# Moving two transfers, one TensorE position and the second half's products inside the steps of a fused attention and RWKV stage

## The chip, the core and the metric

The kernel runs on one core of one Trainium2 chip. The metric is the device time of one launch in microseconds (us), of the only core. TensorE, VectorE, ScalarE, GpSimd and SyncE are called PE, DVE, ACT, POOL and SP, as in the profile; each executes its own list of instructions in order and waits for the others on semaphores.

## The reference, cut to what matters

The program is two transformer-like blocks over 2048 tokens of width 1024. The first block (`hybrid_layer`) normalizes x, multiplies by `w_in`, runs five mixers of 256 columns each, and ends in

```python
mixed = jnp.concatenate([y.astype(x.dtype) * jax.nn.silu(z) for y, z in branches], axis=-1)
return x + mixed @ w_out          # 2048x1280 @ 1280x1024, plus the old x
```

Two of the five mixers stand in the stage of this change. `forgetting_attention` ("Fox") is causal softmax attention with 4 heads of 64, over blocks of 128 queries, so that block k sees (k+1)*128 keys. `rwkv7_time_mix` is a recurrence over tokens,

```python
sa = jnp.einsum("bhvk,bhk->bhv", state, -kk_t)
state = (state * w_t[:, :, None, :] + sa[..., None] * (kk_t * a_t)[:, :, None, :]
         + v_t[..., None] * k_t[:, :, None, :])
```

which the kernel computes in chunks of 128 tokens: running sums of the log decay within the chunk (the "decay sums"), products of scaled rows, and the inverse of a triangular matrix in seven doubling levels. The second block is outside this change.

## The kernel before

The stage is `fox_rwkv_and_gating` (L1062). Its loop runs k from 0 to 17; each k is one **step**, a block in which all engines start together and that ends when all are done. In step k (2 <= k <= 15) these branches run side by side: `rwkv_front` of tile k, `rwkv_back` of tile k-1, `fox_attend` of query block k, `fox_prepare` and `sgu_tile` of tile k+1, `out_product` of tile k-2 (the product with `w_out`) and, up to k = 14, `out_turn` of tile k-1 (its transposes).

**The order of the work is written by hand.** Every branch is a generator per engine; it yields a number between 0 and 1 and then issues instructions. `together` (L162) always continues the branch with the smallest number. The numbers are places in the engine's list, not times: an engine executes its list strictly in that order and stops at each semaphore wait that is not yet met.

**The product** (`out_product`, L1360). For each half n of the 1024 columns, ten blocks j of 128 rows, and a = 0 (the high part of the weights, two 128x512 matmuls) or a = 1 (the low part, one matmul): 40 slices of 256 KB, each loaded by SP into one of five buffers `ow`. The load of slice q is issued when slice q-5 has been used (`o_used`). From step 3 on the first five slices have been loaded in the step before (`ow_ahead`). The places are given by `at(n, j, a)`; in steps 3 and later the first half lies at 0 to 0.025 for slices 0 to 5 and then at 0.08 to 0.38, the second half at 0.405 to 0.775. Each half ends with a DVE addition to the tile's x rows in `ox` (L1436). SP issues from the same loop, ahead of the load of a given slice, the store of the rows of the tile before (L1387, 512 KB) and, after a wait for that store, the load of the old x rows (L1391, 512 KB). The second DVE addition must be done before the transposes of `out_turn` at place 0.84 write the same bank (L1331).

**The RWKV front on PE** (`rwkv_front`, L2404, N = 76). Low-rank products at 8/N; the decay sums at 14/N (L2579 to L2584), which wait for `la_done`, signalled by DVE at 13/N (after L2498), which itself waits for a Tanh of ACT (L2444). ACT takes the exponentials of the sums at 15/N (L2453 to L2455), DVE makes the scaled rows at 17/N (L2509 to L2514), PE turns them from 20/N (L2590). The seven levels follow from place 0.447 on: level l at (34 + 5.5 l + d)/N, with first products at d = -0.6, an ACT copy (L2469) at d = 1.5 and second products at d = 2 (all L2564).

**Places between 14/N = 0.184 and 16/N = 0.211 on PE** hold work of other branches:

| place | work | waits for |
|---|---|---|
| 0.192 | logits of Fox head 1, piece 0 (L1679) | its bank |
| 0.200 | `rwkv_back`'s U products (L2699) | `r_done`, an ACT copy (L2644) at 0.150 |
| 0.208 | turn of head 0, piece 0 (L1703), in steps 12 to 15 only | `f_exps`, ACT's exponential of head 0 (L1619) at 0.175 |
| 0.209 | slice 12 (j = 6, a = 0) of the product (L1424, L1425) | its load |

In steps 9 to 11 (three pieces of 512 keys) the turn of piece 0 is at 0.214.

Of the kernel before, what the change touches and what calls it, by code (L numbers as in the profile page):

```python
# [1211 lines left out]
OUT_K = MIX1 // P  # L1212
# [147 lines left out]
def out_product(c, b, s, t, ahead):  # L1360


    tok = slice(t * P, (t + 1) * P)
    mS, x, wr, bank = b.mS, b.x, b.wr, b.bank
    arrived = (s.ow_in0, s.ow_in1, s.ow_in2, s.ow_in3, s.ow_in4)
    slices = [(n, j, a) for n in range(2) for j in range(OUT_K) for a in range(2)]
    halves = x[:].rearrange("p (n c) -> p n c", n=2)
    cols = lambda n: slice(n * 512, (n + 1) * 512)

    def at(n, j, a=0):  # L1370

        if n == 0 and j < 3 and ahead:
            return 0.0002 * j if (j, a) != (2, 1) else 0.025
        if n == 0 and ahead:
            return 0.08 + 0.3 * (j - 3 + 0.4 * a) / (OUT_K - 3)
        return 0.005 + 0.4 * n + 0.37 * (j + 0.4 * a) / OUT_K

    def sync(sp):
        yield 0.0
        if not ahead:  # L1380
            for q in range(OUT_SLOTS):
                weights(sp, q, arrived[q])
        for q in range(OUT_SLOTS, len(slices)):
            n, j, a = slices[q - OUT_SLOTS]
            yield at(n, j, a) + 0.004
            if q == OUT_K and t:
                sp.dma_start(b.x_out[(t - 1) * P:t * P, :], x[:]).then_inc(s.ox_stored, 16)  # L1387
            if q == OUT_K + 5:
                if t:
                    sp.wait_ge(s.ox_stored, 16)  # L1390
                sp.dma_start(x[:], b.x_old[tok, :]).then_inc(s.ox_in, 16)  # L1391

            sp.wait_ge(s.o_used, q - OUT_SLOTS + 1)
            weights(sp, q, arrived[q % OUT_SLOTS])
        yield at(1, OUT_K) + 0.02
        if t + 3 < TILES:
            sp.wait_ge(s.o_used, len(slices))
            for q in range(OUT_SLOTS):
                weights(sp, q, s.ow_ahead)
            yield 1.0  # L1400
            sp.wait_ge(s.ow_ahead, 16 * OUT_SLOTS)

    def weights(sp, q, signal):
        n, j, a = slices[q]
        sp.dma_start(wr[:, q % OUT_SLOTS].bitcast(F32), b.split_d[OUT_ROWS[j], a, :, cols(n)]).then_inc(signal, 16)

    def landed(pe, q):
        if not ahead:
            pe.wait_ge(arrived[q % OUT_SLOTS], 16 * (q // OUT_SLOTS + 1))
        elif q >= OUT_SLOTS:  # L1410

            pe.wait_ge(arrived[q % OUT_SLOTS], 16 * (q // OUT_SLOTS))

    def tensor(pe):
        for n in range(2):
            for j in range(OUT_K):
                q = (n * OUT_K + j) * 2
                yield at(n, j)
                if j == 0 and n == 1:

                    pe.wait_ge(s.o_added, 1)
                landed(pe, q)
                whi, wlo = wr[:, q % OUT_SLOTS], wr[:, (q + 1) % OUT_SLOTS]
                pe.matmul(bank, mS.hi[:, j], whi, start=(j == 0), stop=False)  # L1424
                pe.matmul(bank, mS.lo[:, j], whi, start=False, stop=False).then_inc(s.o_used, 1)  # L1425
                yield at(n, j, 1)
                landed(pe, q + 1)
                pe.matmul(bank, mS.hi[:, j], wlo, start=False, stop=(j == OUT_K - 1)).then_inc(s.o_used, 1)

    def vector(dve):  # L1430
        for n in range(2):
            yield at(n, OUT_K) + 0.01
            dve.wait_ge(s.o_used, 2 * OUT_K * (n + 1))
            if n == 0:
                dve.wait_ge(s.ox_in, 16)
            dve.tensor_tensor(halves[:, n], halves[:, n], bank, ALU.add).then_inc(s.o_added, 1)  # L1436

    return {"sync": sync, "tensor": tensor, "vector": vector}


# [963 lines left out]
def rwkv_front(c, B, s, proj, i):  # L2404
# [17 lines left out]
    N = 76.0  # L2422
# [136 lines left out]
    def blocks(pe, l, out, left, right, corner):  # L2559

        m = None
        for h in range(HEADS):
            for k, rows, cols in corner if l == LEVELS - 1 else HALVES:
                m = pe.matmul(out[rows, h * P + cols.start:h * P + cols.stop], left(h)[k, rows], right(h)[k, cols],  # L2564
                              start=True, stop=True)
        return m

    def tensor(pe):
        yield 6 / N
        pe.wait_ge(s.lows, 1)  # L2570
        pe.transpose(b1[0:RANK, 0:P], x[:, D_WLO:D_WLO + RANK], c.ident)
        pe.transpose(b1[0:RANK, P:2 * P], x[:, D_ALO:D_ALO + RANK], c.ident).then_inc(s.low_ps, 1)
        yield 8 / N
        pe.wait_ge(s.low_kept, 1)
        pe.matmul(b2[:, 0:GW], loT[:, 0], lo2[:, 0], start=True, stop=True)
        pe.matmul(b2[:, GW:2 * GW], loT[:, 1], lo2[:, 1], start=True, stop=True).then_inc(s.wa_ps, 1)
        yield 14 / N
        pe.wait_ge(s.la_done, 1)
        pe.matmul(b0[:, 0:GW], c.all[:, CENTRED], wa[:, 0], start=True, stop=True)  # L2579
        pe.matmul(b0[:, GW:2 * GW], c.all[:, CENTRED_BEFORE], wa[:, 0], start=True, stop=True)  # L2580
        for j in range(2):
            lj = wa[:, 0, j * P:(j + 1) * P]
            pe.matmul(b1[:, 2 * j:2 * j + 1], lj, c.upto[:, P // 2 - 1:P // 2], start=True, stop=True)
            m = pe.matmul(b1[:, 2 * j + 1:2 * j + 2], lj, c.after[:, P // 2 - 1:P // 2], start=True, stop=True)  # L2584
        m.then_inc(s.cums, 1)
        for j in range(2):
            yield (20 + j) / N
            pe.wait_ge(s.tilde, 1)
            for a in range(4):
                m = pe.transpose((b2, b1)[j][:, a * P:(a + 1) * P],  # L2590
                                 (tl01[:, a] if a < 2 else tl23[:, a - 2])[:, j * P:(j + 1) * P], c.ident)
            m.then_inc((s.turned_a, s.turned_b)[j], 1)
        for j in range(2):
            yield (25 + 4 * j) / N

            pe.wait_ge(s.kept_a, 1)
            pe.wait_ge(s.kept_b, 1)
            if j:
                pe.wait_ge(s.g_done, 2)
            for b in range(2):  # L2600
                for r in range(2):
                    o = slice(HD * r, HD * r + HD)
                    m = pe.matmul(B.big[:, r, b * GW:(b + 1) * GW], XT23[o, j, b],
                                  XT01[o, j].rearrange("p a t -> p (a t)"), start=True, stop=True)
                    if b:
                        m.then_inc(s.grams, 1)
        for l in range(LEVELS):
            yield level(l, -0.6 if l else 0)
            if l == 0:
                pe.wait_ge(s.g_done, HEADS)  # L2610
                pe.wait_ge(s.x_set, 1)
            else:
                pe.wait_ge(s.x_kept, l)
            blocks(pe, l, b0, lambda h: own[:, h], lambda h: X[:, h], [(LOW, HIGH, LOW)]).then_inc(s.p1, 1)
            if l:
                yield level(l, 2)
                pe.wait_ge(s.p1c, l)
                pe.wait_ge(s.xt_kept, l)
                if l < LEVELS - 1:
                    blocks(pe, l, b1, lambda h: XT[:, h], lambda h: Pm[:, h], None).then_inc(s.x_ps, 1)  # L2620
                blocks(pe, l, b2, lambda h: Pm[:, h], lambda h: XT[:, h], [(HIGH, LOW, HIGH)]).then_inc(s.xt_ps, 1)
# [1332 lines left out]
```

## Time and profile before

| | |
|---|---|
| median of 3 runs | 4982.17 us (4981.24, 4982.17, 5010.14) |
| profiled execution | 4980.74 us, span 4979.1 us, mean granted PE clock 0.865 |
| busy share of the span | PE 85%, PE weight loads 63%, DVE 53%, ACT 39%, POOL 15% |
| DMA | 585.32 MB, mean 118 GB/s |
| the stage's steps 0 to 15 | from 1239.8 us on; step 15 begins at 2383.7 us |

A row of a timeline is: start in us, duration in us, engine, line, operation, written and read tiles, shapes, count; in brackets the idle time before it on that engine and what ended it. "PEq L134" is the block boundary. `fox_big` is PSUM, `halves` the split weights of `w_out`. A row of a table of windows is: window and its length, then busy time and count per engine, the granted PE clock (1.00 is 2.4 GHz, 0.50 is 1.2 GHz), the DMA share and GB/s.

### The profile page before, as it was taken

The numbers are of one execution on the slowest core, as the hardware profiler recorded it, in microseconds if no ns is written. First come the engines' busy times: TensorE is split into PE (matmuls) and PEld (weight loads), VectorE is DVE, ScalarE is ACT, GpSimd is POOL, SyncE is SP. The second block draws the span as 40 slices with busy tenths as digits, with TensorE's granted clock in tenths as the row PEclk, the third lists the DMA queues.
The fourth block names the chain that finished last, engine by engine and source line by source line (L and its number), as shares of the span: only waits on it lengthen the run. The fifth ranks groups of instructions, "written<-read, shape, count | busy, mean of one in ns | idle before, by whom it ended". The sixth has DMA issues, their size and how long they took to land. (4 is left out here: it accounts for less than half of the span.)

```text
span 4979.1 us, 66174 instructions
## 1 busy us (share of the span) xinstructions
PE 4215.4 (85%) x23522; PEld 3122.5 (63%) x23522; DVE 2660.2 (53%) x5590; ACT 1936.3 (39%) x4022; POOL 735.7 (15%) x755
## 2 busy tenths in 40 slices
PE   7997998985688898889889999877888787877589
PEld 5885777775566666666668888833444444544467
DVE  3113444444666555555421111178889888888546
ACT  3112232323333333333311101035677767767721
POOL 3111111110100000000000000022223333434500
PEclk9998999996589898989899999966578887788789
DMA  5326666664466555545452212210000001010033
GB/s 181 125 113 221 208 214 212 213 216 145 154 206 205 192 188 167 175 159 162 126 178 85 83 66 72 63 52 19 20 20 20 20 20 39 20 39 18 32 140 114
DMA packets 293737, 585.32 MB, mean 118 GB/s; under 512 B 47944, under 2 KB 80364, under 8 KB 293244
## 3 DMA queue, kind: packets, MB, share of 16 engines
q1 hardware_dynamic: 293408, 581.10, 34.7%
q8 instruction: 187, 3.06, 0.2%
q14 instruction: 142, 1.16, 0.1%
HBM read 453.03 MB, written 127.94 MB: 117 GB/s over the span
## 5 line engine op out<-in xcount | busy, mean ns | idle before, releaser
L3059 PE MATMUL ds_big<-ds_ikT,ds_iqT 64*128 64x512 f32 (+3 forms) x608 | 383.2, 761 | 73.6 <-ACT ds_iqT L3036 53.9
L3526 POOL TENSOR_TENSOR ds_E<-ds_bT 128x256 f32<-128x256 f32 x112 | 72.1, 644 | 2380.9 <-ACT ds_bT L3495 2206.1
L301 PE MATMUL g_acc<-g_ws_hi,g_hT_hi 128*128 128x512 f32 (+1 forms) x1024 | 386.2, 377 | 0.0
L302 PE MATMUL g_acc<-g_ws_lo,g_hT_hi 128*128 128x512 f32 (+1 forms) x1024 | 384.6, 376 | 0.0
L303 PE MATMUL g_acc<-g_ws_hi,g_hT_lo 128*128 128x512 f32 (+1 forms) x1024 | 384.6, 376 | 0.0
L529 PE MATMUL mm_big<-mm_gw_hi,mm_ghT_hi 128*128 128x512 f32 (+1 forms) x768 | 319.8, 416 | 30.3 <-PEq L134 30.3
L3115 DVE TENSOR_SCALAR_CACHE_REDUCE ds_seen<-ds_eq,ds_num 128x2048 uint16<-128x2048 uint16 (+13 forms) x224 | 331.3, 1479 | 26.1 <-issue 4.2
L531 PE MATMUL mm_big<-mm_gw_hi,mm_ghT_lo 128*128 128x512 f32 (+1 forms) x768 | 301.4, 392 | 0.0
L530 PE MATMUL mm_big<-mm_gw_lo,mm_ghT_hi 128*128 128x512 f32 (+1 forms) x768 | 300.5, 391 | 0.0
L3155 ACT ACTIVATE ds_signs<-ds_lo,ds_at 128x2048 bf16<-128x2048 uint16 (+13 forms) x224 | 291.3, 1301 | 2.1 <-issue 0.7
L328 DVE COPY g_stage<-g_acc 128x512 f32<-128x512 f32 (+1 forms) x64 | 41.5, 649 | 459.2 <-PE g_acc L303 459.2
L3022 DVE SCALAR_TENSOR_TENSOR ds_score<-ds_rel,ds_iw,ds_score 128x512 f32<-128x512 f32 (+3 forms) x266 | 219.5, 829 | 54.9 <-ACT ds_rel L3043 37.8
L3059 PEld LDWEIGHTS ds_big<-ds_ikT,ds_iqT 64*128 64x128 f32 x608 | 108.2, 235 | 209.7 <-issue 84.1
L347 ACT ACTIVATE g_stage<-g_acc 128x512 f32<-128x512 f32 (+1 forms) x64 | 36.2, 565 | 502.4 <-PE g_acc L303 502.4
L3043 ACT ACTIVATE ds_rel<-ds_big 128x512 f32<-128x512 f32 (+3 forms) x304 | 162.5, 538 | 158.5 <-PE ds_big L3059 85.2
L3634 PEld LDWEIGHTS ds_big<-ds_E 128*128 128x128 f32 x896 | 134.4, 229 | 135.5 <-POOL ds_E L3533 72.6
L303 PEld LDWEIGHTS g_acc<-g_ws_hi,g_hT_lo 128*128 128x128 f32 x1024 | 193.3, 189 | 35.3
L302 PEld LDWEIGHTS g_acc<-g_ws_lo,g_hT_hi 128*128 128x128 f32 x1024 | 193.5, 189 | 34.8
L301 PEld LDWEIGHTS g_acc<-g_ws_hi,g_hT_hi 128*128 128x128 f32 x1024 | 193.5, 189 | 34.6
L3407 PE MATMUL ds_big<-ds_pT,ds_ct 128*128 128x128 f32 x1088 | 169.3, 300 | 53.7 <-ACT ds_pT L3317 53.5
L1635 ACT ACTIVATE fox_pT<-fox_big 128x512 f32<-128x512 f32 (+3 forms) x160 | 85.4, 533 | 323.3 <-PE fox_big L1703 323.1
L1031 PE MATMUL fp_acc<-fp_ws_hi,fp_hT_hi 128*128 128x512 f32 (+1 forms) x528 | 199.2, 377 | 8.8 <-issue 3.6
(550 smaller groups left out, 10083.1 us busy)
## 6 DMA issues: line engine op xcount, KB each, us to landing
fox_ow<-halves SPq DMA_DIRECT2D x600, 256.0 KB, 3.5
mm_ghT_hi<-turned SPq DMA_DIRECT2D x96, 512.0 KB, 4.0
mm_ghT_lo<-turned SPq DMA_DIRECT2D x96, 512.0 KB, 5.3
proj<-g_stage SPq DMA_DIRECT2D x112, 256.0 KB, 2.0
proj<-mm_gstage SPq DMA_DIRECT2D x80, 256.0 KB, 5.0
mm_x<-proj SPq DMA_DIRECT2D x64, 256.0 KB, 3.8
second_raw<-in_w_in SPq DMA_DIRECT2D x56, 256.0 KB, 4.0
proj<-fp_stage SPq DMA_DIRECT2D x48, 256.0 KB, 2.0
```

Of the source, the lines that this page charges most:

```text
L301: pe.matmul(sums, hT.hi[:, k, tile], wt.hi[:, k, 0:width], start=(k == 0), stop=False)
L302: pe.matmul(sums, hT.hi[:, k, tile], wt.lo[:, k, 0:width], start=False, stop=False)
L303: mm = pe.matmul(sums, hT.lo[:, k, tile], wt.hi[:, k, 0:width], start=False, stop=(k == KD - 1))
L529: pe.matmul(sums, b.hT.hi[:, u % 3, k], wt.hi[:, k, 0:width], start=(k == 0), stop=False)
L530: pe.matmul(sums, b.hT.hi[:, u % 3, k], wt.lo[:, k, 0:width], start=False, stop=False)
L531: m = pe.matmul(sums, b.hT.lo[:, u % 3, k], wt.hi[:, k, 0:width], start=False, stop=(k == KD - 1))
L1031: pe.matmul(sums, hT.hi[:, j % 3, n], ws.hi[:, n, at], start=(n == 0), stop=False)
L3022: d = dve.scalar_tensor_tensor(out=score[:, x:x + wd], in0=rel[:, n % 2, 0:wd], scalar=sg, in1=score[:, x:x + wd], op0=ALU.mult, op1=ALU.add)
L3059: pe.matmul(big[:, n % 2, 0:wd], iqT[o, h // 2], b.ikT[o, x:x + wd], start=True, stop=True)\
L3115: dve.tensor_scalar(seen, hi, cand, 0.0, ALU.is_ge, ALU.add, accum_out=count)
L3155: act.activation(signs, lo, ACT.Sign, bias=now, accum_out=sums[:, bit:bit + 1])
L3407: m = pe.matmul(big[:, 5, h * P:(h + 1) * P], b.ct[:, x // P + t], pT[:, (h * NP + p) % 2, t], start=(p == 0 and t == 0), stop=(x + (t + 1 ...
```

## The change

Three edits. (1) In `out_product`'s SP list the store of x leaves ahead of the load of slice 15 instead of slice 10, and the load of x ahead of slice 19 instead of 15 (the loads of the eighth and tenth row block of the first half). (2) The decay sums' place goes from 14/N to 16/N in steps 9 to 15. (3) The places of the second half's slices are spread over 0.415 instead of 0.37: slice (1, j, a) lies at 0.405 + 0.0415 (j + 0.4 a), the last at 0.795, the DVE addition at 0.83, and SP's loads for the next step at 0.84 instead of 0.795.

```diff
@@ out_product, at()
-        return 0.005 + 0.4 * n + 0.37 * (j + 0.4 * a) / OUT_K
+        return 0.005 + 0.4 * n + (0.415 if n else 0.37) * (j + 0.4 * a) / OUT_K
@@ out_product, sync()
-            if q == OUT_K and t:
+            if q == OUT_K + 5 and t:
                 sp.dma_start(b.x_out[(t - 1) * P:t * P, :], x[:]).then_inc(s.ox_stored, 16)
-            if q == OUT_K + 5:
+            if q == OUT_K + 9:
                 if t:
                     sp.wait_ge(s.ox_stored, 16)
                 sp.dma_start(x[:], b.x_old[tok, :]).then_inc(s.ox_in, 16)
@@ rwkv_front, tensor()
-        yield 14 / N
+        yield (16 if i > 8 else 14) / N
         pe.wait_ge(s.la_done, 1)
```

## Rows read from the trace of the kernel before

**Rows 1.** Windows: whole steps 4, 10 and 11; columns as told above.

```profile
1510.76:1578.17 67.41, 58.03 (x538) 42.69 (x539) 43.10 (x114) 24.86 (x58) 0.00 (x0) 0.96 0.64 208
...
1953.42:2035.43 82.01, 73.71 (x618) 53.59 (x619) 46.81 (x121) 30.55 (x62) 0.00 (x0) 0.90 0.53 171
2035.43:2113.80 78.37, 70.14 (x630) 50.29 (x631) 47.27 (x121) 31.29 (x62) 0.00 (x0) 0.96 0.55 179
```

**Rows 2.** Waits of PE, steps 2 to 15: us in total, times, longest.

```profile
PE fox_big L2564 <- ACT fox_ex L2469: 34.0, 30, 2.0
...
PE fox_big L1424 <- DMA fox_ow<-halves: 14.1, 10, 4.9
PE fox_big L2579 <- DVEq L2499: 12.8, 9, 3.1
...
PE fox_big L1428 <- DMA fox_ow<-halves: 8.6, 8, 3.1
...
PE fox_big L2564 <- DVEq L2543: 2.7, 7, 0.4
```

**Rows 3.** Waits of SP, steps 3 to 14: the block boundary.

```profile
SPq L134 <- PEq L134: 31.8, 13, 5.3
```

**Rows 4.** Timeline of PE in step 6: slice 10 of the product.

```profile
1658.31 0.79 PE L1424 MATMUL fox_big<-fox_ow,fox_mS_hi 128*128 128x512 f32 x1 [1.83 <-DMA fox_ow<-halves]
...
1659.75 0.63 PE L2579 MATMUL fox_big<-fox_wa,consts_sb 128*128 128x256 f32 x1
```

**Rows 5.** Timeline of DVE in step 6: the last operation ahead of la_done.

```profile
1659.13 0.28 DVE L2498 TENSOR_SCALAR fox_wa<-fox_wa 128x256 f32<-128x256 f32 x1
```

**Rows 6.** DMA issues in step 4: KB each, median us from issue to landing.

```profile
x<-fox_ox SPq DMA_DIRECT2D x1, 512.0 KB, 7.0
```

**Rows 7.** Timeline of PE in step 13, from the decay sums on.

```profile
2217.98 1.22 PE L2579 MATMUL fox_big<-fox_wa,consts_sb 128*128 128x256 f32 x2 [2.91 <-DVEq L2499]
...
2221.41 2.06 PE L1679 MATMUL fox_big<-second_raw,fox_q 65*128 65x512 f32 x2
2223.26 1.81 PE L2699 MATMUL fox_big<-fox_R,fox_XT 128*128 128x64 f32 x8
2224.86 0.42 PE L1703 MATMUL fox_big<-consts_sb,fox_L 128*128 128x128 f32 x1
```

**Rows 8.** Timeline of ACT in step 13: r_done, then f_exps.

```profile
2219.06 0.36 ACT L2644 ACTIVATE fox_R<-fox_big 128x256 f32<-128x256 f32 x1
2219.68 1.79 ACT L1619 ACTIVATE fox_L<-fox_L,fox_top 128x1792 f32<-128x1792 f32 x1 [0.25 <-DVE fox_top L1657]
```

**Rows 9.** Timelines of PE and ACT in step 10.

```profile
1966.69 0.70 PE L2579 MATMUL fox_big<-fox_wa,consts_sb 128*128 128x256 f32 x2 [1.26 <-DVEq L2499]
...
1967.78 0.36 ACT L2644 ACTIVATE fox_R<-fox_big 128x256 f32<-128x256 f32 x1
```

**Rows 10.** Timelines of PE: slice 33 in step 2, level 3 in step 13.

```profile
1424.49 0.51 PE L1428 MATMUL fox_big<-fox_ow,fox_mS_hi 128*128 128x512 f32 x1 [3.10 <-DMA fox_ow<-halves]
...
2269.62 0.50 PE L1424 MATMUL fox_big<-fox_ow,fox_mS_hi 128*128 128x512 f32 x1
...
2272.58 0.62 PE L2564 MATMUL fox_big<-fox_ex,fox_XT 64*64 64x64 f32 x14 [2.00 <-ACT fox_ex L2469]
```

**Rows 11.** Windows of 14 us, 10.5 us after the start of steps 3 to 8 and 13.

```profile
1453.29:1467.29 14.00, 13.95 (x47) 10.85 (x48) 5.27 (x17) 7.55 (x22) 0.00 (x0) 0.53 0.51 172
1521.26:1535.26 14.00, 12.74 (x87) 10.39 (x89) 5.93 (x20) 7.99 (x23) 0.00 (x0) 1.00 0.74 242
1588.67:1602.67 14.00, 13.22 (x80) 10.50 (x80) 6.60 (x22) 8.43 (x23) 0.00 (x0) 0.88 0.67 229
1656.99:1670.99 14.00, 12.68 (x37) 9.59 (x38) 6.27 (x20) 6.94 (x18) 0.00 (x0) 0.52 0.50 170
1732.36:1746.36 14.00, 13.12 (x36) 9.33 (x37) 6.26 (x20) 7.04 (x18) 0.00 (x0) 0.51 0.53 165
1809.30:1823.30 14.00, 12.82 (x72) 9.37 (x70) 8.16 (x26) 8.96 (x23) 0.00 (x0) 0.88 0.69 211
...
2213.37:2227.37 14.00, 11.09 (x37) 8.42 (x36) 7.96 (x23) 6.68 (x14) 0.00 (x0) 0.64 0.40 135
```

## The prediction

> **What bounds the kernel now.** I read the windows by step first, then the waits of PE, then the timelines of single steps. The windows show PE busy for 58 to 74 us of steps of 67 to 82 us, with a granted clock under 1 [rows 1]. So in this stage PE's list sets the length of a step: its work, its idle gaps, and the time it spends at the lower clock. SP ends earlier: it waits for PE at the block boundary 31.8 us in 13 waits, 2.4 us a step [rows 3]. The waits of PE that the edits touch are few [rows 2]: the weight slices, 14.1 + 8.6 us over 14 steps; the decay sums on DVE, 12.8 us in 9 waits; the levels' second products on ACT's copy, 34.0 us in 30 waits. Everything the change can win or lose directly lies within these 70 us, 1.4% of the time.
>
> The other lever is the clock. Where PE has waited, the windows show half clock for some time: in step 13, after an idle gap of 2.91 us [rows 7], the 14 us window has 0.64, that is 14 x 0.36 x 2 = 10.1 us at 1.2 GHz [rows 11]. Work at half clock takes twice as long, so such a stretch costs half its length, 5 us. Steps 10 and 11 hold nearly the same work, but take 82.01 and 78.37 us at 0.90 and 0.96 [rows 1].
>
> **Edit 1, the store and load of x.** In steps 3 to 9 PE waits at slice 10, the one whose load SP issues right behind the 512 KB store. The row of step 6 is one of seven, and the longest, 1.83 us [rows 4]. Without step 2's 4.9 us the nine waits of L1424 come to 14.1 - 4.9 = 9.2 us [rows 2], of which seven are these, some 8.3 us. After the edit the store is behind slice 14's load, and that wait goes. But what is late next stands 1.44 us behind it on PE: the decay sums. In step 6 they start at 1659.75 [rows 4], while DVE's last operation ahead of `la_done` ends at 1659.13 + 0.28 = 1659.41 [rows 5]. DVE's path there does not pass through the product, so it is not earlier when slice 10 is. PE gains 0.34 us and waits for `la_done` for the rest of the 1.83. In steps 7 to 9 it waits for `la_done` already, so nothing is gained; for each of steps 3 to 6 I take 0.25 us. Sum: **-1.0 us**, bounds -8.3 (if the wait did not move) and 0.
>
> In their new places the transfers have cover. The store took 7.0 us to land [rows 6]; five slots give the load behind it five slices of 0.3 x 67.4 / 14 = 1.44 us [rows 1], 7.2 us, in the shortest step, and more in longer ones. That store landed in a burst that the new place doesn't have. SP's wait for the store holds back only slice 19's load. The x rows are needed after slice 19, at place 0.39. I take 0; upper bound the same 8.3 us again, at slice 15 (rival D).
>
> **Edit 2, the decay sums later in steps 9 to 15.** Meant work to fill the wait: logits, U products, slice 12, and in steps 12 to 15 a turn. But two of these wait themselves, and for later events than `la_done`. Step 13: PE's work ends at 2217.98 - 2.91 = 2215.07 [rows 7]. `r_done` comes at 2219.06 + 0.36 = 2219.42, and head 0's exponentials end at 2219.68 + 1.79 = 2221.47 [rows 8]. The new list stops at the U products until 2219.42 and at the turn until 2221.5. Then come turn and slice (1.7 us, estimated from four transposes and two matmuls at the lower clock) and the sums, 2221.41 - 2217.98 = 3.4 us [rows 7]: done at 2226.6. The old list has sums, logits and U products done at 2224.86 [rows 7], with turn and slice 2226.6. It is a draw; the sums, though, are ready 5 us later for ACT and DVE, whose copies PE needs soon after. I add 0.3 us a step for steps 12 to 14, nothing for step 15.
>
> Steps 9 to 11 have no turn before the sums. Step 10: PE free at 1966.69 - 1.26 = 1965.43; logits at full clock 0.9 us (half the 2223.26 - 2221.41 = 1.85 of rows 7); U products at 1967.78 + 0.36 = 1968.14 [rows 9]. Idle 1.8 us for 1.26: +0.55 us, three times. Sum: **+2.6 us**, bounds -11.8 (every wait of L2579 in steps 9 to 15 gone: 12.8 [rows 2] less some 1.0 in steps 7 and 8) and +5 (0.7 a step).
>
> **Edit 3, the second half spread.** It helps where slice 33 waits behind the RWKV loads (3.10 us in step 2, the longest of 8 waits of 8.6 us in all [rows 2, 10]): its load gets 0.015 of a step, 1 us, more slack. Step 2 gains that 1.0 us, steps 3 and 4 some 0.5 each of shorter waits; in steps 5 and 6 the wait at level 3 takes the gain. I take -2.0. It costs where PE idles for ACT at level 3's second products: 2.00 us in step 13 [rows 10], similar in ten others. Between level 3's first and second products stand slices 34 and 35, 2272.58 - 2.00 - 2269.62 = 0.96 us [rows 10]; at the new places slice 33 stands there, 34 and 35 come after. ACT's copy waits for a Fox exponential whose logits have only one slice fewer ahead of them (0.35 us). So the gap grows by 0.6 us in steps 5 to 15: +6.6. Slices 38 and 39 now stand ahead of level 5 and fill the 0.4 us gaps there, 7 in all, 2.7 us [rows 2]: -2. Sum: **+2.6 us**, bounds -11.3 (8.6 + 2.7, no gap growing) and +6.6 (nothing gained). At the tail nothing moves: the DVE addition still ends ahead of place 0.84, and SP, whose loads for the next step leave some 3 us later, no longer has the gating store queued behind them and keeps most of its 2.4 us margin [rows 3].
>
> **Sum.** 4980.74 - 1.0 + 2.6 + 2.6 = 4984.9 for the profiled execution; the median is 1.4 us above it, so 4986.
>
> The clock I enter at zero. Low stretches follow the gap at 10 to 13 us in steps 3, 5, 6, 7 and 8 and not in step 4 [rows 11], though the gaps are alike. The edits shift gaps by 1 to 2 us but keep their length, so some stretches will go and others appear.
>
> **Rivals.**
>
> A, faster: with slice 10's wait gone PE's clock stays up in steps 3 to 8. The windows have 0.53, 0.88, 0.52, 0.51 and 0.88 in five of them [rows 11], together 14 x 2 x (0.47 + 0.12 + 0.48 + 0.49 + 0.12) = 47 us at half clock, a price of 23.5 us: 4962 if all goes, 4974 for half. For it: the stretches begin where that wait is. Against: the gap stays, now ahead of the sums. This is what the Trainium skill says under "HAM oscillation — how this bites in real kernels" (TensorE: Matmul & The Clock Gate): waits for a DMA between bursts of matmuls throttle the clock, and joining the bursts keeps it up; step 4, with its wait and 1.00, shows that it does not always. Chance 0.22.
>
> B, faster: the sums' wait is covered after all in steps 9 to 15 (-11.8 for +2.6), and the half clock behind it in 12 to 14 goes (3 x 5 us): 4986 - 14.4 - 15 = 4957. Against: `r_done` and `f_exps` in rows 8 are later than `la_done`. Chance 0.12.
>
> C, slower than before: PE's gap for `r_done` in steps 9 to 11, 1.8 us in one piece where it was 1.0 to 1.3, draws the lower clock as in step 13. Price 5 us each in steps 9 and 11, which are little touched now (0.96 for all of step 11 [rows 1]), 1.5 in step 10: 4986 + 11.5 = 4997. It decides where the gap alone lowers the clock. For it: step 10, with the longest gap of the three, has the stretch and step 11 has not. Chance 0.20.
>
> D, slower: slice 15 or 19 takes slice 10's place: +8.3, 4994. Chance 0.08.
>
> **Numbers.** The forecast, each wait moves and the sum is small, has 0.38 and its own range is 4979 to 4993. The range goes down to 4968 (more than half of A) and up to 5002 (C with D's half); what is left out is full A, full B, and C with all of D, under 0.2. A measurement of this kernel can tell about 1%, 50 us, from no change; no case reaches it alone. Faster 0.01, same 0.97, slower 0.02.
>
> **What would show it.** After: no wait for a slice at slice 10, but one of about 1.3 us for `la_done` ahead of L2579 in steps 3 to 8. In steps 9 to 15 no wait at L2579, but PE idle before L2699 until the copy of L2644 ends, and before L1703 in steps 12 to 14. Level 3's gap 2.6 us instead of 2.0 in step 13. The forecast is wrong if L2699 doesn't wait, or if the clock of steps 3 to 8 goes to 1.00 throughout.

## The result and the profile after

The changed kernel is slower: 5005.44 us median (20 runs) against 4982.76 us (20 runs), a ratio of 1.0044, 95% interval 1.0027 to 1.0062, so +22 us (+13 to +31). The forecast, 4986 with 4968 to 5002, was too low: the sign held, the size was several times what was forecast. The profiled execution took 5014.29 us, 9 us above its median, and that of the kernel before 4980.74, 2 us below its own: the two traces lie 33.5 us apart, and sums read from this pair are a little high.

The waits of PE in steps 2 to 15, after the change (us in total, times, longest), answer to [rows 2]:

```profile
PE fox_big L2564 <- ACT fox_ex L2469: 38.8, 33, 2.5
...
PE fox_big L1424 <- DMA fox_ow<-halves: 14.4, 8, 5.3
PE fox_big L2699 <- ACT fox_R L2644: 11.2, 6, 2.3
...
PE fox_big L2579 <- DVEq L2499: 6.3, 4, 2.2
PE fox_big L1703 <- ACT fox_L L1619: 3.0, 3, 1.3
PE fox_big L1679 <- DVE fox_mx L1650: 2.9, 5, 1.3
PE fox_big L1428 <- DMA fox_ow<-halves: 2.2, 3, 1.5
```

Two things are to be seen. The wait for `r_done` that the prediction described is there, 11.2 us at L2699, and level 3's gap has grown to 2.5 us. And the sum of PE's waits has moved little: all its waits in these steps together give 128.5 us, before 119.7. That is 8.8 us more idle time, for a stretch that is 30 us longer. The windows over steps 2 to 15 tell where the rest is. Before:

```profile
1373.90:2464.61 1090.71, 969.08 (x8320) 707.95 (x8320) 633.57 (x1639) 401.20 (x823) 0.00 (x0) 0.90 0.55 177
```

and after:

```profile
1371.30:2491.56 1120.26, 989.93 (x8320) 722.77 (x8320) 635.24 (x1639) 401.19 (x823) 0.00 (x0) 0.88 0.53 172
```

The same 8320 PE instructions are busy for 20.9 us longer, at a granted clock of 0.88 instead of 0.90. DVE and ACT are busy as before. In this pair, then, 20.9 of 29.6 us are PE's own work at half clock. The clock is lower over all executions too: its mean is 0.861 in the 20 of the change, and 0.864, 0.864 and 0.866 for the kernel before in the three comparisons below.

The windows of 14 us, 10.5 us after the start of the steps, show where the clock fell. These are steps 4 and 6, then 9 to 13, after the change; steps 4, 6 and 13 answer to [rows 11]:

```profile
1517.15:1531.15 14.00, 13.85 (x46) 10.78 (x46) 5.86 (x19) 7.38 (x20) 0.00 (x0) 0.53 0.51 165
...
1662.39:1676.39 14.00, 12.49 (x36) 8.93 (x36) 6.58 (x21) 6.94 (x18) 0.00 (x0) 0.54 0.44 149
...
1891.91:1905.91 14.00, 11.71 (x38) 8.52 (x37) 6.75 (x22) 7.15 (x18) 0.00 (x0) 0.63 0.49 164
1973.50:1987.50 14.00, 11.76 (x38) 8.84 (x37) 6.88 (x21) 7.25 (x18) 0.00 (x0) 0.65 0.50 162
2056.13:2070.13 14.00, 11.98 (x41) 9.05 (x40) 7.02 (x22) 7.36 (x18) 0.00 (x0) 0.63 0.48 167
2140.83:2154.83 14.00, 10.13 (x42) 7.25 (x41) 6.86 (x21) 6.08 (x13) 0.00 (x0) 0.76 0.44 149
2230.12:2244.12 14.00, 9.66 (x36) 7.08 (x35) 5.95 (x18) 5.27 (x10) 0.00 (x0) 0.75 0.45 145
```

and steps 9, 10 and 11 before:

```profile
1886.33:1900.33 14.00, 12.83 (x83) 10.14 (x83) 7.56 (x25) 8.95 (x23) 0.00 (x0) 1.00 0.69 228
1963.92:1977.92 14.00, 12.68 (x57) 9.19 (x56) 7.71 (x24) 7.91 (x20) 0.00 (x0) 0.76 0.55 182
2045.93:2059.93 14.00, 12.90 (x79) 9.68 (x78) 8.50 (x26) 9.14 (x23) 0.00 (x0) 1.00 0.65 216
```

Steps 9 and 11 went from no half clock in this window to 14 x 2 x 0.37 = 10.4 us of it each, step 10 from 6.7 to 9.8 us. That is rival C, in all three of its steps. Such windows also change where no gap was added: step 4 is newly at half clock, with a gap of 1.45 us where it had 1.34 (step 6 stays at half clock).

The signs that the prediction named: in steps 3, 5, 7 and 8 PE waits for `la_done` (0.94, 1.90, 2.23 and 1.22 us), as described, but in steps 4 and 6 it still waits 1.5 us for a slice. PE and ACT in step 10 after the change, the answer to [rows 9]:

```profile
1977.71 1.97 PE L2699 MATMUL fox_big<-fox_R,fox_XT 128*128 128x64 f32 x8 [2.24 <-ACT fox_R L2644]
```

```profile
1977.29 0.37 ACT L2644 ACTIVATE fox_R<-fox_big 128x256 f32<-128x256 f32 x1
```

The U products start 0.05 us after the copy they wait for; the gap is 2.24 us in one piece, where it was 1.26 us. In step 13 (compare [rows 7]) PE now waits three times before the sums:

```profile
2232.66 1.13 PE L1679 MATMUL fox_big<-second_raw,fox_q 65*128 65x512 f32 x2 [1.12 <-DVE fox_mx L1650]
2235.99 1.10 PE L2699 MATMUL fox_big<-fox_R,fox_XT 128*128 128x64 f32 x8 [2.20 <-ACT fox_R L2644]
2238.12 1.12 PE L1703 MATMUL fox_big<-consts_sb,fox_L 128*128 128x128 f32 x4 [1.03 <-ACT fox_L L1619]
...
2239.88 1.05 PE L2579 MATMUL fox_big<-fox_wa,consts_sb 128*128 128x256 f32 x2
```

### The profile page after: what moved, and what is told of

The parts are those of the page before. It is cut to its first block and busy times, and to the rows that moved or that the text cites. A ratio compares the mean times of both kernels' runs of the same rounds, so it can differ in the third digit from the quotient of the medians.

```text
span 5012.7 us, 66174 instructions
## 1 busy us (share of the span) xinstructions
PE 4240.6 (85%) x23522; PEld 3142.7 (63%) x23522; DVE 2660.1 (53%) x5590; ACT 1936.7 (39%) x4022; POOL 733.6 (15%) x755
## 5 line engine op out<-in xcount | busy, mean ns | idle before, releaser
L3059 PEld LDWEIGHTS ds_big<-ds_ikT,ds_iqT 64*128 64x128 f32 x608 | 108.4, 235 | 211.7 <-issue 80.6
L3634 PE MATMUL ds_big<-ds_E 128*128 128x128 f32 x896 | 158.6, 332 | 56.8 <-POOL ds_E L3533 39.4
```

Source lines behind the costliest of these rows:

```text
L3059: pe.matmul(big[:, n % 2, 0:wd], iqT[o, h // 2], b.ikT[o, x:x + wd], start=True, stop=True)\
L3634: m = pe.matmul(big[:, 6 + l % 2, h * P:(h + 1) * P], E[:, l % 2, h], E[:, l % 2, h], start=True, stop=True)
```

## The experiments

The theory, G: PE's gap grows only a little, but a longer gap in one piece lowers the clock over the work behind it, and that is most of the loss; its source is edit 2, because the U products wait for a copy that ACT makes after `la_done`. The rivals: X, the moved transfers collide; S, the spread is the cause; L, the sums' late results hold up ACT and DVE, and the clock only goes with it. One more, N, comes with the filler: the low clock has another cause than the gap, such as the DMA or the kind of work. Ratios are against the kernel before on the same chip, with 95% intervals, from 11 or 12 executions of each version (6 for h1, k2 and k4) and 23 to 35 of the kernel before; 0.001 is 5 us.

**Edit 1 alone.**

```diff
-            if q == OUT_K and t:
+            if q == OUT_K + 5 and t:
-            if q == OUT_K + 5:
+            if q == OUT_K + 9:
```

> Edit 1 alone (x rows' store ahead of slice 15, load ahead of slice 19). Theory G (the loss is the gaps of edit 2 and the lower clock they draw): no part of the loss is here; the wait at slice 10 goes or shrinks, a wait for la_done of 1.2 to 1.9 us stands ahead of the decay sums in steps 3 to 8 instead, time -1 us, within 5 us of before. Rival X (the transfers in their new place collide): a third or more of the +22 us is here, with slice waits in steps 3 to 8 not smaller in sum than before's 8.3 us. Rival A of the prediction (clock stays up): -12 to -24 us.

Measured: 0.9998 (0.9982 to 1.0015). Its waits of PE in steps 2 to 15:

```profile
PE fox_big L2579 <- DVEq L2499: 20.9, 13, 3.1
...
PE fox_big L1424 <- DMA fox_ow<-halves: 5.4, 2, 4.7
```

The slices' wait at L1424 fell from 14.1 to 5.4 us, and the wait for `la_done` rose from 12.8 to 20.9 us, in 13 waits instead of 9. 8.7 us went and 8.1 came back a few matmuls later, at no change of the time. Rivals X and A are out for edit 1.

**Edit 2 alone.**

```diff
-        yield 14 / N
+        yield (16 if i > 8 else 14) / N
```

> Edit 2 alone (decay sums at 16/N in steps 9 to 15). Theory G: most of the loss, +12 to +20 us: PE idles 2.0 to 2.3 us ahead of the U products in steps 9 to 13, every one of steps 9 to 14 then has 7 to 10 us at half clock at 15 to 25 us, and steps 12, 13 and 15 are 2 to 3 us longer in structure. If the sums' place is innocent: within 4 us of before.

Measured: 1.0037 (1.0016 to 1.0058), +18 us, +8 to +29. This is the main part of the loss. The granted clock of all executions says what it is made of: its mean is 0.8604 in the 12 of this version and 0.8636 in the 35 of the kernel before on this chip. The time at half clock is 2 x (1 - clock) x the span, 1398 us and 1360 us: 38 us more, which cost half, 19 us (some 7 to 31, an estimate from the spread of the executions). The same windows as above, of its steps 9, 10 and 11:

```profile
1875.47:1889.47 14.00, 12.04 (x37) 8.68 (x37) 6.75 (x21) 7.15 (x18) 0.00 (x0) 0.64 0.53 173
1957.34:1971.34 14.00, 12.07 (x38) 8.78 (x38) 6.88 (x21) 7.26 (x18) 0.00 (x0) 0.65 0.51 171
2042.75:2056.75 14.00, 12.25 (x39) 8.87 (x38) 7.02 (x21) 7.36 (x18) 0.00 (x0) 0.64 0.53 172
```

In 14 us PE does 37 to 39 instructions where it did 57 to 83. In each window stands one gap of 1.6 to 1.9 us, ahead of L2699.

**Edit 3 alone.**

```diff
-        return 0.005 + 0.4 * n + 0.37 * (j + 0.4 * a) / OUT_K
+        return 0.005 + 0.4 * n + (0.415 if n else 0.37) * (j + 0.4 * a) / OUT_K
```

> Edit 3 alone (second half spread to 0.415). Theory G: level 3's gap 2.1 to 2.5 us where it was 1.3 to 2.0, slices 38 and 39 fill the 0.4 us gaps at level 5: +2 to +5 us. Rival S (the spread is the cause: level 3's longer gap draws the lower clock there): +8 us or more, with half clock at 55 to 75 us of most steps.

Measured: 1.0014 (0.9995 to 1.0033), +7 us (-2 to +16), not clear of none, and not clear of rival S's +8 either. Its waits in steps 2 to 15:

```profile
PE fox_big L2564 <- ACT fox_ex L2469: 40.5, 33, 2.5
...
PE fox_big L1428 <- DMA fox_ow<-halves: 1.1, 4, 0.4
...
PE fox_big L2564 <- DVEq L2543: 0.4, 1, 0.4
```

ACT's copies cost 6.5 us more than before's 34.0 us; the prediction had +6.6. The gaps at level 5 went from 2.7 to 0.4 us, as forecast. Rival S is not out: in this profile, taken 20 us above the version's median, the clock is 0.88 over steps 2 to 15, as after the full change, and half clock stands in the middle of the step (from 46 to 75 us) in 10 of the 14 steps, before in 6. Steps 9 and 11, whose decay sums stay where they were, have 0.76 in the windows read above, behind gaps of 1.36 us at L2579. Over its 12 executions the mean clock is 0.8630 against 0.8636, a price of 4 us, within noise.

**Edits 1 and 3 together.** (Both diffs above.)

> Edits 1 and 3 together, decay sums left at 14/N. Theory G: the sum of the two alone, 0 to +6 us, 14 us or more below the full change (+22). If the three edits only lose together: above +12 us.

Measured: 1.0021 (0.9999 to 1.0043), +10 us. That lies above the 0 to +6 expected and below the +12 of a joint loss. The parts add up within noise: +6 us for the two alone, +10 (0 to +21) together, +22 with edit 2 in. The intervals are too wide to say more.

**R copied early, PE's list untouched.** The control for the next two.

```diff
@@ rwkv_back, scalar()
-        yield 6 / N
+        yield 5.6 / N
         act.wait_ge(s.r_ps, 1)
         act.activation(R[:], by_head(first), ACT.Copy).then_inc(s.r_done, 1)
```

> Before with one move on ACT: the copy R (L2644, r_done) at 5.6/40 = 0.140, just ahead of the Tanh block at 0.145, instead of 0.150 behind it; PE's order untouched. Theory G: r_done is about 5 us earlier, but no one waits for it here: within 4 us of before, la_done's gaps of 1.0 to 2.9 us unchanged. Rival: it delays the Tanh by its 0.36 us and costs up to 5 us.

Measured: 0.9995 (0.9984 to 1.0006). No cost of the copy at its earlier place is seen.

**Edit 2 with its blocker taken away.** The diffs of g1 and of edit 2 together.

> Edit 2 with only its blocker taken away: R copied early, sums at 16/N in steps 9 to 15. Theory G: the U products no longer wait; steps 9 to 11 have no gap there, steps 12 to 14 still wait for f_exps at the turn. At least half of edit 2's +18 us goes: 0 to +8 us. Rival L (the sums' late results are the loss): +14 us or more remains.

Measured: 1.0010 (0.9996 to 1.0024), +5 us. Of edit 2's +18 us some 13 (1 to 26) are gone with one ACT instruction at another place, though the sums are as late on PE's list as in edit 2. PE does not wait less: 123.9 us in sum, 122.1 with edit 2 alone. The clock is back: a mean of 0.8646 over the 12 executions, 0.8642 in the 29 of the kernel before. Steps 9 and 10 in the same windows:

```profile
1891.64:1905.64 14.00, 13.32 (x88) 10.42 (x90) 7.60 (x25) 8.73 (x23) 0.00 (x0) 1.00 0.67 224
1968.71:1982.71 14.00, 13.22 (x70) 9.62 (x69) 8.59 (x26) 8.78 (x22) 0.00 (x0) 0.88 0.64 213
```

and its waits in steps 2 to 15, where L2699 no longer stands:

```profile
PE fox_big L1703 <- ACT fox_L L1619: 10.8, 7, 3.5
...
PE fox_big L2579 <- DVEq L2499: 2.7, 4, 1.0
```

What is left of the loss, if it is not noise, goes with the turn's wait for Fox's exponential. The longest, in step 13:

```profile
2226.74 1.11 PE L1703 MATMUL fox_big<-consts_sb,fox_L 128*128 128x128 f32 x4 [3.49 <-ACT fox_L L1619]
```

Behind this gap the window of step 13 has 0.88, that is 3.4 us at half clock, where 2.91 us of gap had 10.1 before. So the length of one gap alone does not tell how long the clock stays low.

**R copied early, sums at 15.5/N in all steps.**

```diff
@@ rwkv_front, tensor() (and rwkv_back, scalar() as in g1)
-        yield 14 / N
+        yield 15.5 / N
         pe.wait_ge(s.la_done, 1)
```

> R copied early, and the decay sums at 15.5/76 = 0.204 in all steps: behind head 1's logits and the U products, ahead of the turn. Theory G: with r_done no longer late, logits and U products (0.9 + 0.8 us at full clock) fill the gap of la_done: gap in steps 9 to 11 gone, in 12 to 14 about 1.3 us; time -3 to -15 us by the clock. Rival L (late sums themselves cost, because ACT and DVE get them later): +5 us or more although PE has no gap there.

Measured: 1.0005 (0.9995 to 1.0015). Theory G had promised -3 to -15 us, rival L +5 or more; neither came. Its waits in steps 2 to 15:

```profile
PE fox_big L2564 <- ACT fox_ex L2469: 36.2, 32, 2.0
...
PE fox_big L1703 <- ACT fox_L L1619: 5.2, 6, 1.8
PE fox_big L2590 <- DVE fox_tl L2514: 3.5, 3, 1.6
PE fox_big L1679 <- DVE fox_mx L1650: 3.2, 3, 1.3
```

The 12.8 us of `la_done` are gone from the list, and some 14 us stand in four other lines; all its waits sum to 120.9 us, before's to 119.7. So rival L has its part: work pulled ahead of the sums makes their results late, and PE waits for those instead. By the moves tried here a gap was moved on this list, not removed.

**Filler (h1).** Before, with matmuls without use ahead of the wait for `la_done`.

```diff
         yield 14 / N
+        for _ in range(3 if i in (12, 13, 14) else 1 if i >= 3 else 0):
+            pe.matmul(b1, c.ident, c.all[:, 0:512], start=True, stop=True)
         pe.wait_ge(s.la_done, 1)
```

> Before, with matmuls without use (identity by 512 constant columns into bank 1, which the sums overwrite) ahead of the wait for la_done: three in steps 12 to 14, one in steps 3 to 11 and 15, each some 0.9 us at full clock. They add work to the reference's. Theory G (the gap lowers the clock): half clock at 15 to 25 us goes in steps 12 to 14 (10 us each, 5 us of time each) and in step 10: -8 to -20 us, at most 3 us of it given back by filler that outlasts its gap. Rival N (the low stretch has another cause, such as the DMA waits or the kind of work ahead): the stretches stay and the time is +2 to +8 us by the added work.

Measured: 0.9959 (0.9943 to 0.9975), -20 us. More work, less time. Step 13 of it, PE; the six records at L2579 are the three fillers, L2581 is the first of the sums:

```profile
2187.69 2.74 PE L2579 MATMUL fox_big<-consts_sb 128*128 128x512 f32 x6
2190.26 0.59 PE L2581 MATMUL fox_big<-fox_wa,consts_sb 128*128 128x256 f32 x2
...
2191.94 1.10 PE L1679 MATMUL fox_big<-second_raw,fox_q 65*128 65x512 f32 x2
2192.88 1.00 PE L2701 MATMUL fox_big<-fox_R,fox_XT 128*128 128x64 f32 x8
```

and the windows of its steps 12 and 13:

```profile
2102.28:2116.28 14.00, 13.45 (x70) 9.04 (x69) 9.95 (x30) 7.88 (x19) 0.00 (x0) 1.00 0.59 186
2185.69:2199.69 14.00, 13.45 (x71) 8.73 (x72) 9.48 (x29) 8.16 (x20) 0.00 (x0) 1.00 0.56 189
```

The sums start when `la_done` comes, 15.1 us into the step as before, but run at full clock: from the first of the sums to the turn it takes 3.46 us (2193.72, the turn's start) where [rows 7] has 6.88. 70 and 71 instructions stand in windows that had 37. With the idle gap ahead of them filled, the same work and more DMA (186 and 189 GB/s, before 135) run at full clock. So in these steps PE's idle gap is what lowers it, not the DMA or the kind of work; rival N is out there. Over the 6 executions the mean clock is 0.869 against 0.864.

**The full change with filler (k1).** Edits 1 to 3, with one filler in steps 3 to 8 and 15, two in 9 to 11, three in 12 to 14, at 14/N, the sums at 16/N.

```diff
-        yield (16 if i > 8 else 14) / N
+        yield 14 / N
+        for _ in range((2 if i < 12 else 3 if i < 15 else 1) if i > 8 else 1 if i >= 3 else 0):
+            pe.matmul(b1, c.ident, c.all[:, 0:512], start=True, stop=True)
+        yield (16 if i > 8 else 14) / N
```

> The full change with useless matmuls (identity by 512 constant columns, some 0.9 us each at full clock) at 14/N on PE: one in steps 3 to 8 and 15, two in 9 to 11, three in 12 to 14. Theory G (three quarters of the change's loss is half clock that the gaps ahead of the decay sums and the U products draw): the stretches at 15 to 25 us of steps 9 to 14 go (some 9 us each, 4.5 us of time each) and part of those of 3 to 8; the time falls from +22 us against before to between -8 and +4, the rest being the change's own +8 us of gaps and late results. Rival L (the late results are the loss, the clock a by-product): above +14 us.

Measured: 0.9991 (0.9971 to 1.0010), -4 us against before, some 26 us below the change without filler. All three edits and all their late results are in this kernel, and it is not above +14, where rival L had it. But filler took 20 us off the kernel before as well; the fair comparison is with h1. Steps 2 to 15 of h1, then of this kernel:

```profile
1360.32:2431.70 1071.38, 963.30 (x8351) 696.53 (x8351) 632.83 (x1636) 400.37 (x823) 0.00 (x0) 0.92 0.56 180
...
1373.40:2453.70 1080.30, 964.65 (x8356) 696.78 (x8356) 633.64 (x1636) 400.21 (x823) 0.00 (x0) 0.93 0.54 179
```

With the clock alike (0.92 and 0.93) PE is busy for 1.4 us longer, against 20.9 without filler, and its waits sum to 116.7 instead of 108.4 us, 8.3 us more, against 8.8 without filler. So the edits' own waits, rival L's part among them, cost 8 to 9 us, and the rest of the stage's loss was the clock. The medians put 16 us (4 to 28) between the two versions; that these 9 us are all of it is not shown.

**Filler in the tail**, alone (k3) and with h1 (k2), in steps 2 to 15.

```diff
             if l:
+                if l == LEVELS - 1 and i >= 2:
+                    yield 0.884
+                    pe.matmul(b1, c.ident, c.all[:, 0:512], start=True, stop=True)
                 yield level(l, 2)
+                if l == LEVELS - 1 and i >= 2:
+                    pe.matmul(b1, c.ident, c.all[:, 0:512], start=True, stop=True)
                 pe.wait_ge(s.p1c, l)
...
+        if i >= 2:
+            yield 0.96
+            for _ in range(2):
+                pe.matmul(b1, c.ident, c.all[:, 0:512], start=True, stop=True)
```

> Before with the filler of h1 and, in steps 2 to 15, four more such matmuls in the tail: one ahead of the second transposes (gap 0.83 us), one ahead of level 6's second products (gap 1.18 us), two at the very end of PE's list (gap at the block boundary 2.2 to 2.7 us). Theory G: each step has 6.8 us at half clock across its boundary, 3.4 us of time; if the tail's gaps draw it, up to 13 x 3.4 = 44 us go, less filler that outlasts its gap (2 us a step at the lower clock): -20 (h1) - 15 to -40 = -35 to -60 us. If the boundary itself draws it: -20 + 0 to +20 us.

Measured: 0.9932 (0.9907 to 0.9958), -34 us, just short of the -35 to -60 us expected.

> The tail's four matmuls alone. Theory G: the difference between k2 and h1 again, -15 to -40 us. If the two places help each other it is less than that.

Measured: 0.9972 (0.9954 to 0.9990), -14 us, equal to the difference of k2 and h1 (-34 + 20) and just short of the -15 to -40 us expected. Windows of 3 us around the boundary of steps 14 and 15, with PE's busy time, its clock and the DMA; before:

```profile
2377.60:2380.60 3.00, 1.83 (x18) 1.00 0.01 3
2380.60:2383.60 3.00, 0.68 (x7) 0.59 0.00 0
2383.60:2386.60 3.00, 2.94 (x7) 0.50 0.20 63
2386.60:2389.60 3.00, 3.00 (x15) 0.77 0.80 206
```

and in k2, where step 15 starts at 2342.1:

```profile
2336.00:2339.00 3.00, 2.69 (x20) 1.00 0.01 3
2339.00:2342.00 3.00, 2.46 (x11) 1.00 0.03 5
2342.00:2345.00 3.00, 2.88 (x11) 1.00 0.32 95
2345.00:2348.00 3.00, 3.00 (x20) 1.00 0.87 265
```

Part of what the boundary gave was lost again: in k3 seven steps have 13.7 us at half clock from some 10 us after their start on, where the kernel before has three (steps 3, 6 and 7). Why was not found.

**Filler at level 3 too (k4)**, the fastest version. Against k2:

```diff
+                if l == 3 and i >= 7:
+                    for _ in range(1 if i == 7 else 2):
+                        pe.matmul(b1, c.ident, c.all[:, 0:512], start=True, stop=True)
                 pe.wait_ge(s.p1c, l)
```

> k2 with one (step 7) or two (steps 8 to 15) matmuls more ahead of level 3's second products, where PE idles 1.3 to 2.0 us. Theory G: those gaps draw 3.4 us of half clock in about half of the steps (at 59 to 76 us), so 4 x 1.7 = -7 us against k2, if the filler fits; no change or +5 us if it pushes the products behind it.

Measured: 0.9917 (0.9895 to 0.9939), -41 us (4941.59 us median). Against k2 it is 7 us less, as expected in size, but the two intervals overlap, so this last gain is not shown.

## Why the prediction failed

**The step that failed** is "The clock I enter at zero". It took the low stretches for something that comes and goes whatever the gap, though C gave the edit's longer gap a price. PE's busy time for the same instructions grew by 20.9 us in steps 2 to 15, by 1.4 us between the two kernels with filler, and edit 2 alone has 38 us more at half clock over all its executions, 19 us of time: that is the size of the missing 17 us. The step's reason, that the edits shift gaps and keep their length, contradicted the prediction's own working for edit 2, which had the gap in steps 9 to 11 grow from 1.26 to 1.8 us. With edit 2 alone it was 1.88 us in step 10, as worked out; in the full change, where PE is there earlier, it was 2.24 us.

**Edit 1: right.** -1.0 us forecast, -1 us (-9 to +7) measured, and the mechanism is seen in its own run: 8.7 us gone at the slices, 8.1 us back at `la_done`. The cover of the moved transfers held in this run (rival D did not happen); in the full change slice waits of 1.5 us were left in steps 4 and 6.

**Edit 2: mechanism right, size wrong.** The wait at `r_done`, a wait at the turn in step 13 and the draw there came as worked out; the wait of 1.1 to 1.3 us at L1679 in steps 12 and 13 was not foreseen. The term of +2.6 us covers the idle time and late results, and the runs put +18 us (+8 to +29) in its place, of which some 13 go when `r_done` comes early. C's price of 5 us for steps 9 and 11 was the right one (10.4 us at half clock each), but C was given 0.20 and stood beside the sum instead of in it. C's whole case, 4997, is still the low end of what was measured: half clock came in other steps too, as in step 14, whose first 19.7 us ran at half clock after the change, where it had been 14.1 of the first 24 us before.

**Edit 3: right within what was measured.** +2.6 us forecast, +7 us (-2 to +16) measured; of its terms, ACT's copies cost 6.5 us more (+6.6 forecast) and level 5 2.3 us less (-2). The first hit is partly luck: level 3's gap grew by 0.3 to 0.6 us in steps 8 to 15, where 0.6 was forecast, not at all in step 7, and by 0.8 and 1.2 us in steps 5 and 6. Whether the +7 holds a loss by the clock is open. At the slices L1428 fell from 8.6 to 1.1 us, and L1424 took over part of it (14.1 to 18.3 us); the rest, 3.3 us, is more than the 2.0 assumed.

**Rival B** fell as argued: covering the wait was not possible while `r_done` came later than `la_done`. Rival A's full price assumed that a wait moved is a wait gone. On the page that A was weighed with, the Trainium skill's "HAM oscillation — how this bites in real kernels" (TensorE: Matmul & The Clock Gate), the trace agrees with the rule: keeping PE busy held the clock at 1.00 in steps 12 and 13, where it had been 0.65 and 0.64. Moving a gap by 1.4 us, as edit 1 does, is not keeping it busy.

## What to carry to other kernels

Where an engine's clock depends on what it did before, price an idle gap with the busy time it makes slower, not by its own length: here 1 us more of gap in one piece cost 5 us in steps 9 and 11, though a gap of 3.49 us elsewhere drew only 3.4 us at half clock, so look at the trace for each. Before moving work ahead of a wait as cover, look up what that work itself waits for, and on which engine's list the signal stands; here one ACT instruction decided whether the cover was cover. Compare the sum of an engine's waits before and after, and its busy time for the same instructions: in the versions without filler here waits mostly changed their place, and what helped was to change what the engine does while it waits.

## What the runs showed that was not expected

Matmuls without use made the kernel 0.41% faster ahead of one wait, and 0.83% (0.61% to 1.05%) with the tail and level 3: at most 2.7 us of useless PE work a place bought back 10 us at half clock. Gaps of 0.83, 1.18 and 2.2 to 2.7 us, with little work between, stand ahead of the boundary of most steps, and the clock was low across every one; with filler in them (k2) it stayed at 1.00 there from step 3 on.

Nor does the clock come back as soon as PE is busy. The first 20 us of step 14 after the change:

```profile
2312.84:2332.84 20.00, 20.00 (x45) 12.78 (x46) 13.05 (x31) 7.26 (x13) 0.00 (x0) 0.51 0.40 124
```

PE is busy all the time by this profile, at half clock; edit 2 alone and edit 2 with the early copy show the same, 20.00 us and 0.51. Some steps also change from one kernel to the next without an edit that touches them (step 4: 1.00 before, 0.53 with edit 2 alone), and what decides that was not found. Single executions of the kernel before lay between 4952.87 and 5014.79 us in the twenty of the result.
